# Sample attention in groups of 8 pages with a running maximum, K turned by VectorE in 32x32 blocks

## What is computed

```python
PAST_LEN, PAGE_SIZE, DEC_BATCH, DEC_SEQ, FOX_HEADS, FOX_HEAD_DIM = 4096, 128, 8, 8, 12, 64

def fox_sample(k_past, v_past, logf_past, q, k, v, logf):
    # k_past, v_past: (B, 4096, 12, 64), gathered from pages of 128 rows by page_table; q, k, v: (B, 8, 12, 64)
    suffix = (lax.cumsum(lp, axis=1, reverse=True) - lp).transpose(0, 2, 1)
    g = jnp.cumsum(logf.astype(F32), axis=1).transpose(0, 2, 1)
    s_past = einsum('bqhd,bkhd->bhqk', q, k_past) * scale + g[..., :, None] + suffix[..., None, :]
    s_new = einsum('bqhd,bkhd->bhqk', q, k) * scale + g[..., :, None] - g[..., None, :]
    s_new = where(causal, s_new, -inf)
    p = softmax(concatenate([s_past, s_new], axis=-1), axis=-1)
    return einsum('bhqk,bkhd->bqhd', p[..., :n_past], v_past) + einsum('bhqk,bkhd->bqhd', p[..., n_past:], v)
```

## Time and profile before

| quantity | value |
| --- | --- |
| median of 3 runs | 2351.64 us (2349.52 to 2354.65) |
| the profiled execution's own time | 2356.48 us |
| its span in the trace | 2354.4 us |
| PE busy over the span | 2188.0 us (93%) |
| DVE busy | 969.5 us (41%) |
| ACT busy | 464.1 us (20%) |
| DMA | 319.49 MB moved |

### The profile page before, as it was taken

How to read it: one execution, slowest core, us unless ns; L and a number is a source line. 1 busy time by engine, 2 the same in 40 slices (tenths; PEclk the granted TensorE clock), 3 DMA queues, 4 the chain that set the end, 5 groups by cost and what they waited for, 6 DMA issues and landing times.

```text
span 2354.4 us, 34734 instructions
## 1 busy us (share of the span) xinstructions
PE 2188.0 (93%) x12587; PEld 1574.5 (67%) x12587; DVE 969.5 (41%) x1959; ACT 464.1 (20%) x1009; POOL 184.3 (8%) x201
## 2 busy tenths in 40 slices
PE   6999788998999999798999999999997899999996
PEld 3777565555555555276777777677775677777774
DVE  4331654443444444244333444332346343344443
ACT  2002453333233332011122000111101112110002
POOL 1000400000000000010000222100000100002221
PEclk9999999999999999799999999999988999999998
DMA  4221106898999999721122222311201112222221
GB/s 157 72 72 37 61 1 210 301 357 317 330 354 326 331 326 342 244 93 40 72 73 98 81 72 72 107 55 53 74 30 56 72 36 92 88 72 72 72 72 40
DMA packets 127940, 319.49 MB, mean 136 GB/s; under 512 B 10236, under 2 KB 10514, under 8 KB 127678
## 3 DMA queue, kind: packets, MB, share of 16 engines
q1 hardware_dynamic: 124258, 304.67, 36.5%
q0 software_dynamic: 3296, 12.96, 1.6%
q10 hardware_dynamic: 252, 0.16, 0.0%
HBM read 309.18 MB, written 8.55 MB: 135 GB/s over the span
## 4 chain that ended last, share of the span: by engine, by line
PE 82%; DMA 6%; DVE 4%; SPq 4%; issue 3%; ACT 1%; ACTq 0%; DVEq 0%
PE ps L807 48%; PE ps L1001 5%; PE ps L1079 4%; DMA work<-in_cache_k 3%; PE ps L1020 3%; PE ps L1144 3%; PE ps L1145 3%; SPq L507 2%; SPq L497 2%; DMA work<-in_cache_v 2%; PE ps L1025 1%; PE ps L729 1%; PE ps L730 1%; PE ps L1052 1%; PE ps L956 1%
## 5 line engine op out<-in xcount | busy, mean ns | idle before, releaser
L807 PE MATMUL ps<-xn,wring 128*128 128x288 f32 x1104 | 294.6, 410 | 17.6 <-DVE xn L1602 15.7
L807 PE MATMUL ps<-work 128*128 128x288 f32 x1152 | 296.8, 411 | 13.6 <-DVE work L1649 7.8
L807 PEld LDWEIGHTS ps<-work 128*128 128x128 f32 x1152 | 222.1, 193 | 76.9 <-issue 14.7
L807 PEld LDWEIGHTS ps<-xn,wring 128*128 128x128 f32 x1104 | 211.6, 192 | 77.7 <-issue 16.5
L807 PE MATMUL ps<-big,wring 128*128 128x288 f32 x944 | 252.3, 411 | 7.6 <-DVE big L2171 7.6
L1001 PE MATMUL ps<-c,work 128*128 128x128 f32 x1536 | 223.0, 284 | 35.2 <-DMA work<-in_cache_k 27.6
L1001 PEld LDWEIGHTS ps<-c,work 128*128 128x128 f32 x1536 | 170.2, 144 | 106.4 <-issue 62.6
L1447 ACT ACTIVATE big<-ps 128x512 f32<-128x512 f32 x256 | 152.8, 597 | 394.5 <-PE ps L1001 393.8
L807 PEld LDWEIGHTS ps<-big,wring 128*128 128x128 f32 x944 | 181.6, 193 | 59.0 <-DVE big L2171 8.5
L1895 DVE COPY big<-ps 128x256 f32<-128x256 f32 x256 | 107.6, 421 | 243.2 <-PE ps L1001 241.1
L1079 PE MATMUL ps<-work,big 128*32 128x256 f32 x1536 | 173.3, 419 | 17.8 <-DMA work<-in_cache_v 16.2
(11 more groups left out here) (344 smaller groups left out, 2560.0 us busy)
## 6 DMA issues: line engine op xcount, KB each, us to landing
work<-in_cache_k SPq DMA_DIRECT2D x256, 384.0 KB, 5.5
work<-in_cache_v SPq DMA_DIRECT2D x256, 384.0 KB, 5.8
wring<-in_w_up SPq DMA_DIRECT2D x16, 2048.0 KB, 8.8
wring<-in_w_down SPq DMA_DIRECT2D x16, 2048.0 KB, 7.7
wring<-in_w_in_odd SPq DMA_DIRECT2D x6, 2048.0 KB, 8.0
wring<-in_w_in_even SPq DMA_DIRECT2D x5, 2048.0 KB, 9.0
wring<-in_w_out_even SPq DMA_DIRECT2D x2, 2048.0 KB, 8.3
wring<-in_w_out_odd SPq DMA_DIRECT2D x2, 2048.0 KB, 8.5
```

The source lines that it names most:

```text
L807: last = mm(bank, w[:, k, :], x[:, k, :], start=k == 0 and not onto, stop=k == 3, skip_group_check=onto)
```

## The change

The phases, the loop and the lag of one sequence go. The work is now 32 groups of 8 pages (`NG`, `GP`), four to a sequence (`GS`), one after the other, with a running maximum: each group's output is added to an accumulator in SBUF that is first scaled down to the new maximum. K is no longer transposed by PE. DVE transposes each page in place in 32x32 blocks; a page is then a 4x4 pattern of blocks in which each quadrant q of 32 partitions holds 32 of the page's keys' feature blocks. PE scores with 16 tiles of 32 rows by 32 columns: column tile c holds three heads, row tile q reads partitions 32q to 32q+31 and writes PSUM bank 4+q. Queries are laid out once for this during prompt attention (`place_queries`). The new tokens of a sequence are scored and weighed first and start its accumulator. The K ring has 12 buffers, the V ring 8. Everything is written out, without hardware loops. The wait for x ahead of the first weights (SP) and ahead of POOL's small loads is new too.

```diff
 @blk.sync
+            sp.wait_ge(sem("x_in"), 32)
             for j in range(5):
                 unit("in0", j)
...
-            phase(0, ending=False, starting=False)
-            phase(1, ending=False)
-            with sp.Fori(2, NB) as c:
-                phase(c)
+            for g in range(NG):
+                for n in range(g * GP, (g + 1) * GP):
...
+                    if n >= KSLOTS:
+                        sp.wait_ge(sem("scored"), (n - KSLOTS) // GP + 1)
+                    sp.dma_start(k_ring[:, k_slot(n), :], rows_of("cache_k", ids[n % 4])).then_inc(k_in[k_slot(n)], 16)
+                for n in range(g * GP, (g + 1) * GP):
...
+                    if n >= VSLOTS:
+                        sp.wait_ge(sem("v_page_used"), n - VSLOTS + 1)
+                    sp.dma_start(v_ring[:, n % VSLOTS, :], rows_of("cache_v", ids[n % 4]))\
+                        .then_inc(v_in[n % VSLOTS], 16)
 @blk.tensor
+            def score_group(g):
+                b = g // GS
+                pe.wait_ge(sem("k_turned"), GP * (g + 1))
...
+                for n in range(2 * HC + 1):
+                    for c in range(CG):
+                        for q in range(4):
+                            r = slice(32 * q, 32 * q + 32)
...
+                            last = mm(ps[32 * c:32 * c + 32, 4 + q, 0:256], w, x, start=(n == 0), stop=(n == 2 * HC))
+                last.then_inc(sem("scored"), 1)
...
+            new_tokens(0)
+            for g in range(NG):
+                score_group(g)
+                if g % GS == 0 and g:
+                    turn_out(g // GS - 1)
+                for u in range(2):
+                    turn_half(g, u)
+                for p in range(GP):
+                    weigh_page(g, p)
+                if g % GS == GS - 2 and g // GS + 1 < NB:
+                    new_tokens(g // GS + 1)
 @blk.scalar
+            def exp_group(g):
+                act.wait_ge(sem("shift_made"), g + 1)
...
+                act_f(probs.rearrange("p (g q k) -> p q g k", g=GP, q=4),
+                      ps[:, 4:8, 0:256].rearrange("p q (g k) -> p q g k", g=GP), ACT.Exp,
+                      bias=shift_s(b, n), accum_out=group_den(b)).then_inc(sem("exp_done"), 1)
 @blk.vector
+            def turn_page(n):
+                slot = k_slot(n)
+                dve.wait_ge(k_in[slot], 16 * (n // KSLOTS + 1))
+                x = k_ring[:, slot, :]
+                nc.vector.transpose(x, x).then_inc(sem("k_turned"), 1)
+            def shift_group(g):
...
+                dve.wait_ge(sem("scored"), g + 1)
+                own(nc.vector.reduce_max(group_max(b), ps[:, 4:8, 0:256], AX.XY, negate=True))
+                own(tt(neg_max(b, n), neg_max(b, n - 1), group_max(b), ALU.min))
+                stt(shift_s(b, n), neg_max(b, n), gate, gate, ALU.subtract, ALU.add).then_inc(sem("shift_made"), 1)
+            def add_out(g):
...
+                dve.wait_ge(sem("v_page_used"), GP * (g + 1))
...
+                stt(o, o, decay(b), ps[:, 3, 0:HC * D], ALU.mult, ALU.add).then_inc(sem("out_added"), 1)
...
+            new_tokens(0)
+            for g in range(NG):
+                turn_bias(g)
+                for p in range(GP):
+                    turn_page(g * GP + p)
+                if g % GS == 0 and g:
+                    place_out(g // GS - 1)
+                shift_group(g)
+                for u in range(2):
+                    take_half(g, u)
+                add_out(g)
+                if g % GS == GS - 1:
+                    scale_out(g // GS)
+                if g % GS == GS - 2 and g // GS + 1 < NB:
+                    new_tokens(g // GS + 1)
```

More of the change, by code:

```diff
@@ L161, in tables @@
         "upto_s": one(same & (q <= g)),
[L162 to L167, removed]
+        "head_of": one(np.arange(H)[:, None] == row_head[None, :]),
+        "mask_new": np.where(g % NS <= p % NS, 0.0, NEG).astype(np.float32),
+        "own_query": one(g % NS == p % NS),
+        "head_row": one(p % 32 == row_head[None, :]),
         "inv_cnt": (1.0 / cnt).astype(np.float32).reshape(P, 32),
@@ L526, in _ @@
-            phase(0, ending=False, starting=False)
-            phase(1, ending=False)
-            with sp.Fori(2, NB) as c:
-                phase(c)
-            phase(NB, k=False)
-            for q in range(PAGES - LAG, PAGES, RING):
-                ids = page_ids(NB - 1, q)
-                for m in range(RING):
-                    page("cache_v", NB - 1, q + m, ids)
+                    ptab[0:1, n:n + 4], engines=[mybir.EngineType.SP], min_val=0, max_val=NPHYS - 1)
+                return ids
@@ L1450, in exps @@
-            def exps(b, c):
-                act.wait_ge(sem("softmax_shift"), b + 1)
-                n = 2 * GROUP * PAGE
-                part = S[:, c * n:(c + 1) * n] if c < EXPS else S[:, c * n:c * n + TS]
-                act_f(part, part, ACT.Exp, bias=sshift, accum_out=ssum[:, c:c + 1]).then_inc(sem("exp_done"), 1)
-            def k_pages(b, soft):
-                for p in range(PAGES):
-                    copy_page(b, p)
-                    if soft is not None and 1 <= p <= EXPS:
-                        exps(soft, p - 1)
-                        if p == EXPS:
-                            exps(soft, EXPS)
@@ L1472, in add_and_square, with exp_new @@
+            def exp_new(b):
+                act.wait_ge(sem("new_shift_made"), b + 1)
+                x = probs_new[:, b, NS * b:NS * b + NS]
+                act_f(x, x, ACT.Exp, bias=shift_s(b, 0), accum_out=den_s(b)).then_inc(sem("new_exp_done"), 1)
+            exp_new(0)
+            for g in range(NG):
+                exp_group(g)
+                if g % GS == GS - 2 and g // GS + 1 < NB:
+                    exp_new(g // GS + 1)
             def add_and_square(k):
@@ L1995, in _ @@
-            own(nc.vector.memset(pTs[:, PAGES, :], 0.0))
-            phase(0, ending=False, starting=False)
-            phase(1, ending=False)
-            with dve.Fori(2, NB) as c:
-                own.loop(c - 2, 6)
-                phase(c)
-            own.end(NB - 2)
-            phase(NB, k=False)
+                for c in range(2):
+                    for i in range(HC):
+                        hd = HC * c + i
+                        at = 64 * (i % 2)
+                        src = ps[at:at + D, 2, i // 2 * P:i // 2 * P + P].rearrange("p (a n) -> p a n", a=2)
+                        to = 64 * (hd % 2)
+                        dst = xn[to:to + D, 2:KD, :].rearrange("p (a f) t -> p f a t", a=2)[:, hd // 2]
+                        ins = cp(dst[:, :, SEQ + NS * b:SEQ + NS * b + NS],
+                                 src[:, :, 32 * c + NS * i:32 * c + NS * i + NS])
+                        if c == 1 and i == HC - 1:
+                            ins.then_inc(sem("turn_taken"), 1)
```

483 lines of the change are left out of this document (198 added, 285 removed).

## The result

The changed kernel takes 2557.05 us (median of 4 runs, 2552.34 to 2558.78); on the same chip the kernel before took 2350.58 us (4 runs, 2346.85 to 2354.65). The ratio is 1.0875, with a 95% interval of 1.0851 to 1.0899: 206 us slower. The forecast was 2581 us.

A forecast was written before the change was run, and what follows sets the result against it. It took a group as one serial chain of DVE, PE and ACT: 32 x 25.1 us plus the work around it, a stage 231 us longer, -2 us elsewhere, forecast 2581 us (own range 2540 to 2620; wider range 2395 to 2810).

The forecast's parts named there:

- main step: Sample attention: each group is one chain of DVE, PE and ACT in turns, nothing of the next beside it; 25.1 us.
- suffix and turning: DVE, each group: eight page transposes at 0.95 us and the suffix at 0.41, together 8.0 us.
- scores, with the hand-over: PE, each group: 14 sets of 16 tiles, 3.2 us at 2.4 GHz or 6.2 at 1.2; 5.6 us taken.
- V pages: PE, each group: 16 sets of four column tiles at 0.32 us at 1.2 GHz, 5.3 us; 2.8 at 2.4 GHz.
- a sign of being wrong: Scores on PE: the prediction is wrong if a set of 16 tiles takes more than 0.43 us.
- 1.2 GHz for nearly all of it: PE in the chain: idle 8.4 us ahead of every score and 3 us behind, it mostly runs at 1.2 GHz.
- 0.50 in most windows: Expected sign in the changed profile: PE's clock at 0.50 in most windows of the stage.
- PE keeps 2.4 GHz: Rival on PE's clock: scores, halves and V pages shrink by 2.4, 0.7 and 2.5 us, 179 us, 2402 us; chance 0.10.
- faster: Rival: chain under 17.9 us, with turning at 0.55 us a page and PE at 2.4 GHz, 2295 us; chance 0.07.
- row tiles don't all run together: Rival on PE's scores: row tiles run in turns; four in turns would give 2800 to 3180 us; chance 0.13.
- No cost: Page transfers in the sample attention: 17.2 us a group lie beside the 25.1 us chain at no cost.
- Elsewhere: Outside the stage: x about 4.5 us earlier at the start, prompt attention 2.5 us longer, together -2 us.

The follow-up runs named there:

- run 1: Changed kernel with DVE turning the next group's suffix and eight K pages ahead of the addition of this group's output: 2463.8 us.
- run 2: Changed kernel with the next group's suffix and K page 0 turned behind the shift, page 1 between the copies, six pages behind the second copy: 2412.0 us.
- run 12: From run 9: K page 4 turned between the two copies, new tokens behind the halves with pages 5 to 7 between their steps: 2332.0 us.
- run 3: Changed kernel plus eight filling matmuls of 512 columns in each group, into a bank that nothing reads: 2514.2 us.
- run 10: Run 3 with only a quarter of each K and V page transferred, all instructions kept: 2484.1 us.
- run 11: Changed kernel with only a quarter of each K and V page transferred, all instructions kept: 2539.8 us.
- run 4: Changed kernel with only 384 of the 768 columns of each K page turned: 2482.8 us.
- run 8: Run 2 with only a quarter of the columns of each K and V page transferred, all instructions kept: 2339.4 us.
- run 9: Run 2 plus V pages weighed one group late, and four K pages of group g+2 turned while PE scores g+1: 2348.4 us.
- Run 6: Kernel before with only the two waits for x added: 2345.8 us, ratio 0.9978.
- run 5: Changed kernel without its two waits for x: 2562.1 us.

## Why the prediction held

**The chain.** It was right in its main step: eight turns ahead of each score with nothing of another group beside them. Runs 1 and 2 moved nothing but DVE's turning and got 93 and 145 us back; run 12, with the same transposes, tiles and running maximum in another order, got back the 206 us of the loss and 19 more.

**The terms.** Means over the 32 groups, in us (for the scores without the seven groups in which DVE places an output before the shift; with them it is 7.3):

| term | predicted | measured |
| --- | --- | --- |
| suffix and turning | 8.0 | 7.4 |
| scores, with the hand-over | 5.6 | 7.0 |
| shift | 1.6 | 1.7 |
| exponential | 1.3 | 1.3 |
| halves | 2.5 | 2.5 |
| V pages | 5.3 | 4.5 |
| adding | 0.4 | 0.3 |
| hand-overs | 0.4 | in the others |
| sum | 25.1 | 24.7 |

The sum was good partly because two terms erred in opposite directions. *Scores* were mis-sized: a set does not cost 0.43 us throughout. Sets at 1.2 GHz started 0.50 us apart in the mean and up to 0.65 where PE did not stop, which is over the 0.43 that the prediction itself named as a sign of being wrong; here it fell on one term alone. *V pages* were sized for 1.2 GHz, and part of them ran at more: the granted clock over them was 0.64 in the mean, 0.52 to 0.71 by group. *Turning* took the row of 1.055 ns an element, which proved right: 935 ns against 0.95, and eight in 6.96 us because the next starts 0.86 us after the last. The new tokens took 4.0 us, not 5.4, in seven groups, and 1.4 x 7 = 10 us of the forecast's excess is that; the first score came 15.5 us into the stage, not 16.6. The stage came to 842 us against 868.

**The clock.** The step that failed is "1.2 GHz for nearly all of it", and with it the sign "0.50 in most windows": the windows show 0.66 to 0.76. PE started each score at 1.2 GHz (granted clock 0.50) after its 7.8 us of idle and reached 2.4 GHz (1.00) before the end of it in all 32 groups. The rival "PE keeps 2.4 GHz" would have been worth 179 us by my numbers; run 3 got 43 us out of the clock and the same filling 56 with a quarter of the bytes (run 10 against 11), neither holding it fully (0.89 over the stage in both), and the scores at best had nowhere near the 3.2 us that I had worked out (next paragraph). The rival "faster" had PE keep 2.4 GHz because it would idle less than 5 us. In run 4 it idled 4.5 to 5.1 us ahead of each score and began 26 of the 32 at a clock of 0.50.

**Packed tiles.** The rival "row tiles don't all run together" held in a milder form. In run 8, in groups with PE at 2.4 GHz throughout and no gap, the first and the last matmul of the 14 sets start 4.27 us apart: 0.305 us a set, 1.45 times the 0.21 of a set of three column tiles (half the 0.43 of 512 columns). One tile alone costs about as much: single matmuls of 288 columns start 0.243 us apart at a clock of 1.00 (L807 of the kernel before), which is 0.216 for 256. So a set of 16 did the work of some 16 / 1.45 = 11.0 tiles in the time of one. Four row tiles in turns would have made 56 sets of the 14, 12 us at 0.21 and 24 at 0.43, and by my numbers a kernel of 2800 to 3180 us; the 4.27 us exclude it. At 1.2 GHz the sets cost 0.50 us in the mean against the 0.43 of one tile (288 columns 0.480, so 256 0.427, at a clock of 0.50), 1.15 times, a gain of 14: 0.44 in the mean of the first four, then 0.55.

**Transfers.** "No cost" was nearly right: 17 us of 2557 (run 11). But it was right only while the chain was slow. At 2412 us they already cost 73 us (run 8): 53 through PE's waits for issue and 10 through late K pages. The prediction did not name that price. It is what run 2 fell short by; runs 1, 9 and 12 show the same waits in the scores (28.0, 29.3 and 38.9 us), but were not run with fewer bytes, so what it cost them is not shown.

**Elsewhere.** Predicted -2 us with the start at -4.5 and prompt attention at +2.5; the first matmul came 4.2 us earlier and the stage began 2.3 us earlier, so what lies between them took 1.9 us more. Run 6 shows the wait for x as the cause of the gain, and run 5 agrees with it.

## What to carry to other kernels

When work moves from one engine to another, cost the new chain before the new load: here PE and ACT had less work over the kernel (2039.9 for 2188.0 us and 321.0 for 464.1) and DVE only 125 us more (1094.5 for 969.5), with slack for it, and the kernel took 9% longer because DVE prepared the next group only after the last step of this one. The same operations in an order where each engine has another group's work while it waits won 1% instead. And once a chain is tightened, look in its waits for a cost that the sum doesn't have: here PE stood still for 57.0 us within its scores, 224 matmuls and as many weight loads a group, at a DMA share of 0.84 (run 2), and for 3.9 us at 0.32 (run 8).

## What the hardware showed that I had not expected

*PE's instructions came late beside the full transfers.* Within a group's scores, 224 matmuls and as many weight loads, PE stopped for up to 3.7 us with nothing to wait for. Over the stage: 6.0 us at a DMA share of about 0.69 (changed kernel), 28.0 at about 0.78 (run 1), 57.0 at 0.84 (run 2), 3.9 with a quarter of the bytes (run 8, share about 0.32).

The single packets of q8, one of the two instruction queues of the trace, 16,384 bytes each, show what PE waited for. Each of the 25 stops of run 2 ended 1.3 to 1.6 us after such a packet had landed, and the stops stand at regular places of PE's program: counted in matmuls and weight loads, they lie whole multiples of 256 apart, to within one. The same holds, with 1.2 to 1.6 us, for every stop of PE of over 0.4 us named "issue" between the first and the last score in the changed kernel and in all its other variants: 154 more, and none in run 11. The packets were not slower in run 2 than in run 8 (1.02 and 1.13 us in the mean); they began later, 1.4 to 4.4 us after PE had started the instruction 256 places ahead of the stop, against 0.6 to 1.1 us in the five stops of run 8. So the instructions were late, and with a quarter of the page bytes they came earlier; why a packet starts late is not shown.

The five pieces of 5.3 us at each loop turn of the kernel before carry the same name and are something else: in the trace they stand between two instructions of SP (L528), and PE works on through them.

*Sets of 16 tiles alternated.* Starts of successive sets of 16 matmuls, from the trace of run 8 in a group at 2.4 GHz: 0.24, 0.22, 0.43, 0.22, 0.39, then 0.24 and 0.38 in turns. In run 11 at 1.2 GHz: 0.43 four times with one of 0.47 between, then 0.63 and 0.43 in turns until the clock rises. The same 181 instructions, at 2.4 GHz (run 8) and for the most part at 1.2 GHz (run 11):

```profile
450.19 3.80 PE L1052 MATMUL ps<-work,big 32*32 32x256 f32 x181 [2.62 <-DVE work L1879]
```

```profile
399.00 5.74 PE L1052 MATMUL ps<-work,big 32*32 32x256 f32 x181 [7.84 <-DVE work L1879]
```

*A 32x32-block transpose on DVE cost what a plain operation did*: 935 ns for 128x768 float32 and 536 ns for 128x384 (run 4), so 1.04 ns an element and 0.14 us besides (128x256 took 436 ns, 0.03 us over that line), against 1.055 ns and 0.14 us in the plain operations of 684 and 1359 ns, and hardly more with PE's scores and full transfers beside it (946 and 957 ns in runs 9 and 12).
